# Delta rule: diagonal squares in the merges of the triangular inverse, and gate rows spread by transfers

## The chip, the cores and the metric

The kernel runs on one core of a Trainium2 chip. TensorE (PE) multiplies matrices, VectorE (DVE), ScalarE (ACT) and GpSimd (POOL) work on elements, SyncE (SP) issues transfers; each engine works through its own instructions in order and waits on semaphores. The metric is the device time of one execution in microseconds (us), lower is better. TensorE reads its operands from SBUF (128 partitions) and writes to PSUM, which has eight banks in every partition; a matmul smaller than the array takes only a square or rectangle of it, named by its rows and columns (128*128, 64*64, 16*16 in the profile's rows).

## The reference

Two transformer blocks over 256 tokens of width 1024, all in float32. The first has stick-breaking attention, an MLP, retention and another MLP. The second puts 16 meta tokens in front (272 tokens), and mixes with two branches, a gated delta rule and a forgetting attention, and ends with a layer of experts that are gathered from memory. The change lies in the gated delta rule. Cut to what matters, per head:

```python
G = jnp.cumsum(g, axis=-1)
gamma = jnp.where(incl, jnp.exp(G[:, None] - G[None, :]), 0.0)
k_beta = k * beta[..., None]
a_mat = jnp.where(strict, k_beta @ k.T * gamma, 0.0) + jnp.eye(CHUNK)
rhs = jnp.concatenate([v * beta[..., None], k_beta * jnp.exp(G)[..., None]], axis=-1)
sol = triangular_solve(a_mat, rhs, left_side=True, lower=True, unit_diagonal=True)
q_dec = q * jnp.exp(G)[..., None]
```

## The kernel before, in words

The weights stream from memory in 1 MB blocks of 128x2048 float32, issued by SP in `sync_blocks` (L576) into two slots in turn. ACT makes the upper part of each half-block (`weights_hi`, L602), DVE the rest (`weights_lo`, L611), and PE multiplies in three products (L625, L626, L627). SP may issue block b only when DVE has made the lower part of block b-2, since it goes to the same slot.

The delta rule comes after the convolution (`conv` blocks) and works on 8 heads in 2 groups of 4, over three token tiles of 16, 128 and 128 tokens (`TILES`). `tensor_delta`, `scalar_delta`, `vector_delta` and `gpsimd_delta` are the four engines' shares of it, written out in order by hand. Between the steps stand numbered fill points: at those in `DELTA_POINTS` each engine does half a block of the projections that the forgetting attention, the gates and so on need (24 matmuls of PE into bank 7). In group 0 no fill stands at points 10, 12, 16, 18 and 25; in group 1, of points 9 to 19, only at 14 and 17. Fill point 6+2L lies between the two products of level L, and 7+2L behind them.

The gates' rows G, beta and exp(G) lie in `lam`, one head to a partition (0 to 7), 272 tokens along it. ACT copies six of its rows to partitions 32, 64 and 96 (`scalar_spread`, three transfers). In each group PE spreads each of the three rows over all 128 partitions with a matmul by a 0/1 matrix (`tensor_pick`, L1586; four heads, on four row tiles and in four banks), and DVE reads it from PSUM: `dgam` (L2076), `dkb` (L2086), `dlast` and `dqe` (L2090, L2091).

The unit lower triangular matrix of each 128-token tile is inverted by merging: at level L, blocks of size 2^L on the diagonal are joined in pairs. A level does, for each tile and head, a transpose (L1952), the product M of the masked matrix `dB` and the second halves of `dTT` (L1959, 64 moving columns), copies of M and of the transpose to SBUF by ACT (L2044, L2046), the product Z (L1970), and a subtraction by DVE (L2130) into `dTT`; POOL masks `dA` into `dB` for the next level when M has been made (L2179). The products use the whole 128x128 array, although only squares on the diagonal carry anything. Level 6, the last, works on 64x64 quarters (L1950, L1957, L1968, `whole`). The 16-token tile (names ending in m) takes part up to level 3.

## Time and profile before

| | us |
|---|---|
| median of 3 runs | 1841.1 (1838.98 to 1842.49) |
| profiled execution | 1846.39 |
| its span | 1845.1 |
| PE busy | 1705.1 (92%) |
| DVE busy | 1187.9 (64%) |
| ACT busy | 752.1 (41%) |
| POOL busy | 400.0 (22%) |
| L1959 on the whole array, x160 | 20.1 |
| L1970 on the whole array, x160 | 20.1 |
| L1586 in the delta rule, x48 | 4.4 |

A float32 matmul appears as two records on PE, each of the three products of a half-block as one. The delta rule lies between about 806 and 1000 us of the span. Busy time is the time with something of that group running; the distance from one group's start to the next is what it takes on the engine. The clock that a window shows is 1.00 for TensorE's upper level (2.4 GHz) and 0.50 for its lower (1.2 GHz).

### The profile page before, as it was taken

The numbers are of one execution on the slowest core, as the hardware profiler recorded it, in microseconds if no ns is written. First come the engines' busy times: TensorE is split into PE (matmuls) and PEld (weight loads), VectorE is DVE, ScalarE is ACT, GpSimd is POOL, SyncE is SP. The second block draws the span as 40 slices with busy tenths as digits, with TensorE's granted clock in tenths as the row PEclk, the third lists the DMA queues.
The fourth block names the chain that finished last, engine by engine and source line by source line (L and its number), as shares of the span: only waits on it lengthen the run. The fifth ranks groups of instructions, "written<-read, shape, count | busy, mean of one in ns | idle before, by whom it ended". The sixth has DMA issues, their size and how long they took to land.

```text
span 1845.1 us, 23154 instructions
## 1 busy us (share of the span) xinstructions
PE 1705.1 (92%) x9262; PEld 1296.8 (70%) x9262; DVE 1187.9 (64%) x2131; ACT 752.1 (41%) x1324; POOL 400.0 (22%) x343
## 2 busy tenths in 40 slices
PE   8999999999999999999999999988788788878888
PEld 7979988977799888989999989863333333333333
DVE  5676654765566547864262666689777766777855
ACT  4655533444355436774363655442222121122211
POOL 0220000000000000002012000335545544544551
PEclk9999999999999999999899999998989878988899
DMA  6336555444455553532231224799999999999997
GB/s 252 135 117 213 189 184 183 176 167 160 160 182 184 183 183 137 183 118 79 82 115 47 107 100 173 283 382 418 422 421 421 422 421 421 422 421 421 421 422 311
DMA packets 62955, 453.85 MB, mean 246 GB/s; under 512 B 7000, under 2 KB 7128, under 8 KB 8448
## 3 DMA queue, kind: packets, MB, share of 16 engines
q0 software_dynamic: 37152, 268.45, 35.1%
q1 hardware_dynamic: 25040, 178.27, 27.0%
q10 hardware_dynamic: 656, 5.66, 0.9%
q8 instruction: 73, 1.20, 0.3%
q14 instruction: 34, 0.28, 0.0%
HBM read 451.15 MB, written 1.05 MB: 245 GB/s over the span
## 4 chain that ended last, share of the span: by engine, by line
PE 68%; DMA 14%; DVE 8%; ACT 4%; POOL 3%; issue 2%; another core or an unknown queue 0%; DVEq 0%; ACTq 0%; POOLq 0%
PE banks L625 16%; PE banks L627 16%; PE banks L626 16%; DMA uv_rows<-expert_uv,index 14%; PE banks L2539 10%; DVE uv_rows L2725 3%; POOL uv_rows L2755 3%; ACT weights_hi L602 1%; PE banks L1970 1%; PE banks L1959 1%; DVE weights_lo L611 1%; PE banks L1690 1%; PE banks L1952 1%; ACT diag L2604 1%; PE banks L2313 0%
## 5 line engine op out<-in xcount | busy, mean ns | idle before, releaser
L2539 PE MATMUL banks<-uv_rows,diag 128*128 128x512 f32 x1024 | 509.0, 660 | 110.2 <-ACT diag L2604 110.2
L611 DVE TENSOR_TENSOR weights_lo<-weights,weights_hi 128x1024 fp32r<-128x1024 f32 x325 | 397.1, 1263 | 252.0 <-ACT weights_hi L602 252.0
L2539 PEld LDWEIGHTS banks<-uv_rows,diag 128*128 128x128 f32 x1024 | 214.6, 213 | 403.2 <-issue 273.1
L602 ACT ACTIVATE weights_hi<-weights 128x1024 fp32r<-128x1024 f32 x328 | 328.9, 1052 | 357.4 <-PE banks L627 340.9
L625 PE MATMUL banks<-x_hi,weights_hi 128*128 128x256 f32 (+1 forms) x1472 | 426.6, 290 | 5.0 <-DVE weights_lo L611 1.4
L627 PE MATMUL banks<-x_hi,weights_lo 128*128 128x256 f32 (+1 forms) x1472 | 419.7, 285 | 0.0
L626 PE MATMUL banks<-x_lo,weights_hi 128*128 128x256 f32 (+1 forms) x1472 | 419.3, 285 | 0.0
L2725 DVE CUSTOM_DVE_ANT_0 uv_rows<-uv_rows,tokens 128x1024 f32<-128x1024 f32 x256 | 305.5, 1223 | 147.1 <-DMA uv_rows<-expert_uv,index 147.0
L2755 POOL DMA_INDIRECT uv_rows<-expert_uv,index x254 | 315.5, 1242 | 309.2 <-PE banks L2539 256.1
L625 PEld LDWEIGHTS banks<-x_hi,weights_hi 128*128 128x128 f32 x1472 | 281.1, 191 | 12.1 <-DVE weights_lo L611 3.1
L627 PEld LDWEIGHTS banks<-x_hi,weights_lo 128*128 128x128 f32 x1472 | 280.9, 191 | 0.0
L626 PEld LDWEIGHTS banks<-x_lo,weights_hi 128*128 128x128 f32 x1472 | 280.0, 190 | 0.5 <-issue 0.2
L2598 ACT ACTIVATE coef<-act_in 128x8 f32<-128x8 f32 (+3 forms) x43 | 8.9, 207 | 375.4 <-DVE act_in L2725 375.4
L625 PE MATMUL banks<-weights_hi,mlp_hi 128*128 128x512 f32 x256 | 101.2, 395 | 0.0
L627 PE MATMUL banks<-weights_hi,mlp_lo 128*128 128x512 f32 x256 | 101.0, 395 | 0.0
L626 PE MATMUL banks<-weights_lo,mlp_hi 128*128 128x512 f32 x256 | 101.0, 395 | 0.0
L2604 ACT ACTIVATE diag<-sb_now,coef 128x128 f32<-128x128 f32 x256 | 79.5, 388 | 14.7 <-DVE coef L2735 14.7
L835 POOL TENSOR_SCALAR stat<-stat 128x1 f32<-128x1 f32 x6 | 1.2, 207 | 357.4 <-DVE stat L813 357.2
L625 PE MATMUL banks<-weights_hi,x_hi 128*128 128x512 f32 x160 | 65.6, 410 | 1.8 <-DVE weights_lo L611 1.8
L626 PE MATMUL banks<-weights_lo,x_hi 128*128 128x512 f32 x160 | 63.4, 397 | 0.0
L627 PE MATMUL banks<-weights_hi,x_lo 128*128 128x512 f32 x160 | 63.4, 396 | 0.0
L627 PEld LDWEIGHTS banks<-weights_hi,mlp_lo 128*128 128x128 f32 x256 | 48.2, 188 | 11.2
(384 smaller groups left out, 2073.4 us busy)
## 6 DMA issues: line engine op xcount, KB each, us to landing
weights<-weights SPq DMA_DIRECT2D x164, 1024.0 KB, 4.8
uv_rows<-weights SPq DMA_DIRECT2D x4, 1024.0 KB, 7.7
uv_rows<-expert_uv,index POOLq DMA_INDIRECT x254, 17.5
sb_first<-constants_first ACTq DMA_DIRECT2D x1, 1920.0 KB, 9.5
sb_always<-constants_always ACTq DMA_DIRECT2D x1, 1627.5 KB, 7.2
sb_peer<-constants_peer ACTq DMA_DIRECT2D x1, 1544.0 KB, 8.0
h<-x SPq DMA_DIRECT2D x1, 1024.0 KB, 5.8
out<-h SPq DMA_DIRECT2D x4, 256.0 KB, 4.6
```

The lines of the kernel that those rows point to most:

```text
L602: self.act.activation(self.w_hi[b % SLOTS][:, f], raw[:, f], ACT.Copy).then_inc(self.hi_made, 1)
L611: self.dve.tensor_tensor(self.w_lo[b % SLOTS][:, f], self.landing(b)[0][:, f], self.w_hi[b % SLOTS][:, f], ALU.subtract).then_inc(self.lo_ ...
L625: self.pe.matmul(out, wh, xh, start=first, stop=False)
L626: self.pe.matmul(out, wh, xl, start=False, stop=False)
L627: return self.pe.matmul(out, wl, xh, start=False, stop=last)
L1690: mm = self.pe.matmul(self.bank(2 * (c % 3) + j, width), self.C["ones"][:, :], squares[:, j, :], start=True, stop=True)
L1952: pe.transpose(turned[:, hh * n:(hh + 1) * n], tt[:, hh, :], C["ident"][0:n, 0:n])
L1959: mm = pe.matmul(ps[:, hh], b[:, hh, :], self.second(tt, lvl)[:, hh], start=True, stop=True)
L2539: mm = pe.matmul(self.bank(2 * t + half), self.diag[:, k, :], self.uv[ROW_BUFFER[n]][:, f], start=(u < NT and k == 0), stop=(u >= UNITS - ...
L2604: act.activation(self.diag[:, k, :], self.C["ident"][:, :], ACT.Copy, scale=self.coef[:, u, k:k + 1]).then_inc(self.diags, 1)
L2725: dve.tensor_tensor_reduce(rows, rows, self.tokens[:, t, :], 1.0, 0.0, ALU.mult, ALU.add, self.act_in[:, u, k:k + 1]).then_inc(self.dots, 1)
L2755: pool.indirect_dma_start(self.uv[ROW_BUFFER[n]][:, :], None, self.ins["expert_uv"], bass.IndirectOffsetOnAxis(ap=self.index[:, u, k:k + 1 ...
```

## The change

In `tensor_delta`, levels 2 to 5 of the two 128-token tiles (`parted`) do M and Z as squares on the diagonal: at levels 2, 3 and 4 four squares of 32x32 with 16 moving columns, at level 5 two of 64x64 with 32. All squares of a head write one bank, each its own partitions. Level 1, level 6, the transposes and the 16-token tile stay.

The rows of G, beta and exp(G) are spread by SP instead (`sync_spread`): in each group, for each of the four heads, one transfer takes beta and G (2176 bytes of one partition) to all 128 partitions of the new buffer `drows`, and one takes exp(G) (1088 bytes) to rows of `lam` that are no longer needed. They stand ahead of one weight block each time (`SPREAD_AT`). The picks in the delta rule are gone; DVE reads the rows from SBUF and waits until all eight transfers of the group have landed. ACT copies only one row now (`ncum`, for the forgetting attention), in one transfer. `drows` lies where the gates' first half will be, so ACT's first gates fill waits for DVE's last read of it.

```diff
--- before.py
+++ after.py
@@ -194,6 +194,8 @@
           ("ret_out", 8), ("mlp_up1", 16), ("mlp_down1", 16), ("conv", 12), ("fa_qkv", 12), ("delta_z", 4),
           ("gates", 8), ("branch_a", 4), ("branch_b", 4), ("mix_out", 4), ("queries", 8))
 N_BLOCKS = sum(n for _, n in STREAM)
+CONV_AT = sum(n for _, n in STREAM[:10])
+SPREAD_AT = (CONV_AT + 9, CONV_AT + 12 + 8)
 HALVES = {"sb_v": 2, "sb_out": 2, "mlp_down0": 2, "ret_out": 2, "mlp_down1": 2, "mix_out": 2}
 SQUARES = (("sb", 1, 1), ("mlp0", 1, 1), ("ret", 1, 1), ("mlp1", 1, 1), ("meta", 1, 0), ("peer", 1, 1))
 ROOTS = (("sb", 2), ("ret", 2), ("meta", 1), ("mixer", 2), ("final", 2), ("peer", 2))
@@ -380,6 +382,9 @@
         self.branch.append([self.place(f"branch_{n}1", [P, KD, SM], F32R) for n in ("hi", "lo")])
         self.top = at
         self.fa_qkv = self.place("fa_qkv", [P, 3 * H2, SM])
+        at = self.top
+        self.d_rows = self.place("drows", [P, HG, 2, SM])
+        self.top = at
         self.y[0], self.y[1] = self.place("gates_a", [P, KD, S]), self.y[0]
@@ -573,6 +578,8 @@
                 self.sync_ahead(own + 1)
             if b >= SLOTS:
                 self.sp.wait_ge(self.lo_made, PARTS * (b - SLOTS + 1))
+            if b in SPREAD_AT:
+                self.sync_spread(SPREAD_AT.index(b))
             self.sp.dma_start(self.raw[b % SLOTS][:, :], w[b]).then_inc(self.block_full[b % SLOTS], 16)
         self.sync_ahead(own + 2)
         self.sync_ahead(own + 3)
@@ -1572,13 +1579,32 @@
     def row(self, name):
         return self.lam[0:H2, self.LAM.index(name), :]
-    LAM = ("beta", "G", "nbe", "tail", "eG", "ncum", "y", "t", "u", "g")
+    LAM = ("nbe", "tail", "beta", "G", "eG", "ncum", "y", "t", "u", "g")
+    SPREAD = 16 * 2 * HG
+
+    def sync_spread(self, group):
+
+        sp, beta, eg, kept = self.sp, self.LAM.index("beta"), self.LAM.index("eG"), self.LAM.index("ncum") + 1
+        if group == 0:
+            sp.wait_ge(self.lam_ready, 1)
+            sp.wait_ge(self.lam_eg, 1)
+            sp.wait_ge(self.h_normed, NT)
+        else:
+            sp.wait_ge(self.d["rows_used"].sem, self.d["rows_used"].at(0, 3))
+        for hh in range(HG):
+            h = group * HG + hh
+            sp.dma_start(self.d_rows[:, hh], self.lam[h:h + 1, None, beta:beta + 2, :].to_broadcast([1, P, 2, SM])).then_inc(self.rows_spread, 16)
+            sp.dma_start(self.lam[:, kept + hh, :], self.lam[h:h + 1, None, eg, :].to_broadcast([1, P, SM])).then_inc(self.rows_spread, 16)
+
+    def rows_landed(self, group):
+
+        return self.rows_spread, 16 + (group + 1) * self.SPREAD
     def scalar_spread(self):
+        at = self.LAM.index("ncum")
         self.act.wait_ge(self.lam_ready, 1)
-        for j in range(1, 4):
-            self.act.dma_start(self.lam[j * QUARTER:j * QUARTER + H2, 0:6, :], self.lam[0:H2, 0:6, :]).then_inc(self.rows_spread, 16)
+        self.act.dma_start(self.lam[QUARTER:QUARTER + H2, at, :], self.lam[0:H2, at, :]).then_inc(self.rows_spread, 16)
     def tensor_pick(self, out, name, h, quarter, width, start=True):
@@ -1823,6 +1849,16 @@
         return t > 0 and lvl == self.LEVELS[t] - 1
+    def parted(self, lvl, t):
+
+        return t > 0 and lvl > 1
+
+    def parts(self, lvl):
+
+        n = max(QUARTER, 2 << lvl)
+        for at in range(0, P, n):
+            yield slice(at, at + n), slice(at >> lvl + 1, at + n >> lvl + 1), slice(at // 2, (at + n) // 2)
+
     def level_count(self, lvl, t):
         return sum(len(self.active(l)) for l in range(1, lvl)) + self.active(lvl).index(t) + 1
@@ -1861,6 +1897,8 @@
         name, s, sub, b = self.fill(i)
         c = 2 * s + sub
         act.wait_ge(*self.fill_made(i))
+        if name == "gates" and c == 0:
+            act.wait_ge(self.d["rows_used"].sem, self.d["rows_used"].at(1, 3))
         if name == "fa_qkv":
             act.activation(self.fa_qkv[:, c, :], self.bank(FILL_BANK, SM), ACT.Copy).then_inc(self.fill_moved, 1)
         elif name == "delta_z":
@@ -1898,17 +1936,9 @@
         def fill(point):
             self.fill_point(self.tensor_fill, group, point)
-        if group == 0:
-            pe.wait_ge(self.rows_spread, 16 * 3)
-        for j, name in enumerate(("G", "beta", "eG")):
-            if j:
-                wait("rows_used", j)
-            for hh in range(HG):
-                h = group * HG + hh
-                mm = self.tensor_pick(self.bank(hh, SM), name, h, hh, SM)
-            mm.then_inc(d["rows"].sem, 1)
+        for j in range(3):
             fill(j)
-        wait("rows_used", 3)
+        wait("rows_used", 2)
         if group == 0:
             pe.wait_ge(self.conv_silu, self.st["conv"].n)
         for t, (c, n) in enumerate(TILES):
@@ -1955,6 +1985,9 @@
                 for hh in range(HG):
                     if self.whole(lvl, t):
                         mm = pe.matmul(ps[0:half, hh, 0, :], a[half:P, hh, 0:half], tt[half:P, hh, half:P], start=True, stop=True)
+                    elif self.parted(lvl, t):
+                        for x, blocks, cols in self.parts(lvl):
+                            mm = pe.matmul(ps[x, hh, blocks], b[x, hh, x], self.second(tt, lvl)[x, hh, blocks], start=True, stop=True)
                     else:
                         mm = pe.matmul(ps[:, hh], b[:, hh, :], self.second(tt, lvl)[:, hh], start=True, stop=True)
                 mm.then_inc(d["M"].sem, 1)
@@ -1966,6 +1999,10 @@
                 for hh in range(HG):
                     if self.whole(lvl, t):
                         mm = pe.matmul(pzt[0:half, hh, 0, :], tm[0:half, hh, 0:half], m1[0:half, hh, 0:half], start=True, stop=True)
+                    elif self.parted(lvl, t):
+                        for x, blocks, cols in self.parts(lvl):
+                            mm = pe.matmul(pzt[x, hh, blocks], tm[x, hh, x], m1[x, hh, cols].rearrange("p (b s) -> p b s", s=1 << lvl),
+                                           start=True, stop=True)
                     else:
                         mm = pe.matmul(pzt[:, hh], tm[:, hh, :], m1[:, hh, 0:n // 2].rearrange("p (b s) -> p b s", s=1 << lvl),
                                        start=True, stop=True)
@@ -2027,8 +2064,8 @@
             act.wait_ge(d["turn"].sem, d["turn"].at(group, t + 1))
             for hh in range(HG):
                 h, f = group * HG + hh, slice(hh * P, (hh + 1) * P)
-                act.activation(self.d_ktail[0:n, t, f], self.bank(2)[0:n, f], ACT.Copy, scale=self.token_scalar(t, 3, h))
-                made = act.activation(self.d_bv[0:n, t, f], self.bank(3)[0:n, f], ACT.Copy, scale=self.token_scalar(t, 0, h))
+                act.activation(self.d_ktail[0:n, t, f], self.bank(2)[0:n, f], ACT.Copy, scale=self.token_scalar(t, 1, h))
+                made = act.activation(self.d_bv[0:n, t, f], self.bank(3)[0:n, f], ACT.Copy, scale=self.token_scalar(t, 2, h))
             made.then_inc(d["turn_used"].sem, 1)
             fill(3 + t)
             act.wait_ge(d["back"].sem, d["back"].at(group, t + 1))
@@ -2069,12 +2106,12 @@
         def fill(point):
             self.fill_point(self.vector_fill, group, point)
-        rows = self.banks(0, HG, SM)
-        wait("rows", 1)
+        beta, rows = self.d_rows[:, :, 0, :], self.lam[:, self.LAM.index("ncum") + 1:, :]
+        dve.wait_ge(*self.rows_landed(group))
         for t, (c, n) in enumerate(TILES):
             for hh in range(HG):
-                g = dve.tensor_scalar(self.d_gam[0:n, hh, c:c + n], self.bank(hh)[0:n, c:c + n],
-                                      self.token_scalar(t, 1, group * HG + hh), 0.0, ALU.subtract, ALU.min)
+                g = dve.tensor_scalar(self.d_gam[0:n, hh, c:c + n], self.d_rows[0:n, hh, 1, c:c + n],
+                                      self.token_scalar(t, 3, group * HG + hh), 0.0, ALU.subtract, ALU.min)
                 if (t, hh) != (2, HG - 1):
                     step.of(g)
         g.then_inc(d["rows_used"].sem, 1)
@@ -2082,10 +2119,10 @@
             for i in CONV_FILLS:
                 self.vector_fill(i)
         fill(0)
-        wait("rows", 2)
-        dve.tensor_tensor(self.d_kb[:, :, :], k, rows, ALU.mult).then_inc(d["rows_used"].sem, 1)
+        if group == 0:
+            dve.wait_ge(self.rms_scaled.sem, self.rms_scaled.at("conv", 8))
+        dve.tensor_tensor(self.d_kb[:, :, :], k, beta, ALU.mult).then_inc(d["rows_used"].sem, 1)
         fill(1)
-        wait("rows", 3)
         for t, (c, n) in enumerate(TILES):
             step.of(dve.tensor_copy(last[:, :, t:t + 1], rows[:, :, c + n - 1:c + n]))
         dve.tensor_tensor(self.d_qe[:, :, :], q[:, :, META:SM], rows[:, :, META:SM], ALU.mult).then_inc(d["rows_used"].sem, 1)
@@ -2291,6 +2328,7 @@
         for i in range(H2 + 2):
             if i < H2:
                 if i == 0:
+                    pe.wait_ge(*self.rows_landed(1))
                     pe.wait_ge(self.rms_read.sem, self.rms_read.at("outs", 12))
                     pe.wait_ge(self.rms_scaled.sem, self.rms_scaled.at("outs", 8))
                 if i >= 2:
```

PE at level 2 of group 0, before (`dTTm`, `dMm` belong to the 16-token tile; a row with x3 counts matmuls of the other heads; 1959 is M, 1952 the transpose, 1970 Z):

```order
L1952 MATMUL banks<-sb_now,dTT 128x128 [waits d_T]
L1952 MATMUL banks<-sb_now,dTT 128x128 x3
L1959 MATMUL banks<-dTT,dB 128x64 [waits d_B]
L1959 MATMUL banks<-dTT,dB 128x64 x3
L1970 MATMUL banks<-dMm,dTm 16x8 [waits d_M1]
L1970 MATMUL banks<-dMm,dTm 16x8 x3
L1970 MATMUL banks<-dM,dT 128x64 [waits d_M1]
L1970 MATMUL banks<-dM,dT 128x64 x3
```

The same place after (M is L1990, the transpose L1982, Z L2004):

```order
L1982 MATMUL banks<-sb_now,dTT 128x128 [waits d_T]
L1982 MATMUL banks<-sb_now,dTT 128x128 x3
L1990 MATMUL banks<-dTT,dB 32x16 [waits d_B]
L1990 MATMUL banks<-dTT,dB 32x16 x15
L2007 MATMUL banks<-dMm,dTm 16x8 [waits d_M1]
L2007 MATMUL banks<-dMm,dTm 16x8 x3
L2004 MATMUL banks<-dM,dT 32x16 [waits d_M1]
L2004 MATMUL banks<-dM,dT 32x16 x15
```

Each set of 4 matmuls has become one of 16; what stands around them, and what they wait for, is as it was.

SP at the first spread, after; before, the two weight blocks (`weights_49` and `weights_50` are the two slots) follow each other with a wait for `block_lo_made` each:

```order
L583 DMA weights_49<-weights 128x2048 [waits block_lo_made]
L1596 DMA drows<-lam 128x1x544 [waits lam_eg,h_normed,lam_ready,block_lo_made]
L1597 DMA lam<-lam 128x1x272
L1596 DMA drows<-lam 128x1x544
L1597 DMA lam<-lam 128x1x272
L1596 DMA drows<-lam 128x1x544
L1597 DMA lam<-lam 128x1x272
L1596 DMA drows<-lam 128x1x544
L1597 DMA lam<-lam 128x1x272
L583 DMA weights_50<-weights 128x2048
```

Eight transfers stand between two blocks, and the first waits for the gates' rows; the block that used to be next is now behind them in the same queue.

PE at the first pick of group 0, before:

```order
L627 MATMUL banks<-x_hi,weights_lo_54 128x272
L1586 MATMUL banks<-lam,sb_always 128x272 [waits rows_spread,rms_read]
L1586 MATMUL banks<-lam,sb_always 128x272 x3
L625 MATMUL banks<-x_hi,weights_hi_52 128x272 [waits half_blocks_moved]
L626 MATMUL banks<-x_lo,weights_hi_52 128x272
L627 MATMUL banks<-x_hi,weights_lo_54 128x272
```

And after, where the products (L632 to L634) follow one another:

```order
L632 MATMUL banks<-x_hi,weights_hi_52 128x272
L633 MATMUL banks<-x_lo,weights_hi_52 128x272
L634 MATMUL banks<-x_hi,weights_lo_54 128x272
L632 MATMUL banks<-x_hi,weights_hi_52 128x272 [waits half_blocks_moved,rms_read]
L633 MATMUL banks<-x_lo,weights_hi_52 128x272
L634 MATMUL banks<-x_hi,weights_lo_54 128x272
```

The four picks and their wait for `rows_spread` are gone, and the wait for bank 7 stands with the product.

## Rows read from the trace of the kernel before

**Rows 1.** The page: busy time, chain of waits, one kind of transfer.

```profile
PE 1705.1 (92%) x9262; PEld 1296.8 (70%) x9262; DVE 1187.9 (64%) x2131; ACT 752.1 (41%) x1324; POOL 400.0 (22%) x343
...
GB/s 252 135 117 213 189 184 183 176 167 160 160 182 184 183 183 137 183 118 79 82 115 47 107 100 173 283 382 418 422 421 421 422 421 421 422 421 421 421 422 311
...
PE 68%; DMA 14%; DVE 8%; ACT 4%; POOL 3%; issue 2%; another core or an unknown queue 0%; DVEq 0%; ACTq 0%; POOLq 0%
...
weights<-weights SPq DMA_DIRECT2D x164, 1024.0 KB, 4.8
```

**Rows 2.** Windows: stretch, length, busy time and count by engine, granted clock, DMA share, GB/s.

```profile
813.30:816.70 3.40, 3.40 (x17) 3.40 (x16) 2.85 (x3) 2.27 (x4) 0.00 (x0) 0.50 0.86 299
892.00:895.10 3.10, 2.09 (x27) 1.63 (x25) 0.00 (x0) 2.92 (x6) 0.00 (x0) 1.00 0.00 0
895.10:902.00 6.90, 6.90 (x38) 6.78 (x39) 3.10 (x4) 0.43 (x2) 0.00 (x0) 0.51 0.16 46
998.80:1004.40 5.60, 4.82 (x55) 3.97 (x55) 0.83 (x2) 2.26 (x6) 0.00 (x0) 1.00 0.52 187
```

**Rows 3.** Timeline of PE, group 1, level 2: start, length, engine, line, operation, tile, count.

```profile
975.12 0.61 PE L1952 MATMUL banks<-sb_now,dTT 128*128 128x128 f32 x4
975.56 1.00 PE L1959 MATMUL banks<-dTT,dB 128*128 128x64 f32 x8
976.49 0.35 PE L1970 MATMUL banks<-dMm,dTm 16*16 16x8 f32 x8
976.78 2.00 PE L1970 MATMUL banks<-dM,dT 128*128 128x64 f32 x16
978.71 0.26 PE L1952 MATMUL banks<-sb_now,dTTm 16*16 16x16 f32 x4
```

**Rows 4.** Timeline, group 0, level 2: ScalarE's copies and GpSimd's masks.

```profile
859.04 2.56 POOL L2179 TENSOR_TENSOR dB<-dA,sb_always 128x512 f32<-128x512 f32 x2 [1.12 <-PE banks L1959]
...
859.28 0.59 ACT L2046 ACTIVATE dT<-banks 128x512 f32<-128x512 f32 x1
...
860.56 0.59 ACT L2046 ACTIVATE dT<-banks 128x512 f32<-128x512 f32 x1
```

**Rows 5.** Timeline of PE, group 0, level 6.

```profile
892.41 0.68 PE L1957 MATMUL banks<-dTT,dA 64*64 64x64 f32 x8
893.02 0.41 PE L1950 MATMUL banks<-sb_now,dTT 64*64 64x64 f32 x4
```

**Rows 6.** Windows of 0.02 us: L978 (two column tiles, one bank).

```profile
67.70:67.72 0.02, 0.02 (x2) 0.02 (x2) 1.00 1.54 410
```

**Rows 7.** Windows of 0.02 us: L1586 (four row tiles, four banks).

```profile
806.52:806.54 0.02, 0.02 (x4) 0.02 (x4) 1.00 0.00 0
```

**Rows 8.** Timeline of PE at the second and third row spread, group 0.

```profile
812.73 0.39 PE L625 MATMUL banks<-x_hi,weights_hi 128*128 128x272 f32 x1 [1.41 <-DVE weights_lo L611]
...
817.47 0.74 PE L1586 MATMUL banks<-lam,sb_always 8*128 8x272 f32 x8
818.14 0.39 PE L625 MATMUL banks<-x_hi,weights_hi 128*128 128x272 f32 x1
```

**Rows 9.** Timelines of SP, ACT and PE: two weight blocks from issue to use.

```profile
756.36 0.33 SPq L576 DMA_DIRECT2D weights<-weights  x1
...
764.76 2.01 ACT L602 ACTIVATE weights_hi<-weights 128x1024 fp32r<-128x1024 f32 x2 [0.30 <-PE banks L627]
...
770.91 0.29 PE L625 MATMUL banks<-x_hi,weights_hi 128*128 128x272 f32 x1
...
845.48 0.33 SPq L576 DMA_DIRECT2D weights<-weights  x1
...
865.86 1.99 ACT L602 ACTIVATE weights_hi<-weights 128x1024 fp32r<-128x1024 f32 x2
```

**Rows 10.** Transfers, 756.0 to 757.2: only lam's copy moves.

```profile
DMA packets 19, 0.05 MB, mean 44 GB/s; under 512 B 11, under 2 KB 11, under 8 KB 19
...
weights<-weights SPq DMA_DIRECT2D x1, 1024.0 KB, 6.0
```

More of the change, by code:

```diff
@@ L525, in signals @@
         self.rows_spread = nc.alloc_semaphore("rows_spread")
-        names = {"rows": 3, "rows_used": 3, "gam": 3, "prod": 3, "prod_used": 3, "turn": 3, "turn_used": 3, "masked": 3, "attn": 2,
+        names = {"rows_used": 3, "gam": 3, "prod": 3, "prod_used": 3, "turn": 3, "turn_used": 3, "masked": 3, "attn": 2,
                  "back": 3, "A": 3, "T0": 3, "B": 13, "M": 15, "M1": 15, "Z": 15, "T": 15, "ks": 2,
@@ L2139, in vector_delta @@
                 for hh in range(HG):
-                    x = dve.scalar_tensor_tensor(self.d_rhs[:, H[hh]], ks[:, H[hh]], self.token_scalar(t, 2, group * HG + hh),
+                    x = dve.scalar_tensor_tensor(self.d_rhs[:, H[hh]], ks[:, H[hh]], self.token_scalar(t, 0, group * HG + hh),
                                                  self.d_bv[:, t, H[hh]], ALU.mult, ALU.add)
```

## The prediction

> **What bounds the kernel now.** I read the page first: PE is busy for 1705.1 of the span and carries 68% of the chain of waits [rows 1], so a microsecond taken from PE's row is a microsecond of the kernel unless something else arrives late there. Then the windows around the delta rule: PE is full in most of it, and the exceptions are level 6 of the inverse, where it is busy for 2.09 of 3.10 us and for 4.82 of 5.60 us [rows 2]. The reader should see in the same group that the granted clock stands at 0.51 for the 6.90 us behind the first of these, and at 0.50 for 3.40 us at 813.3: the lower of the two levels, after a stretch in which PE paused or stood. Last the timelines: how long one set of a level takes on PE, and when ScalarE and GpSimd deliver what the next set needs.
>
> **The squares.** Five steps give the sum.
>
> First, a whole-array set of 4 matmuls (8 records): the second M set of level 2 runs from 975.56 to 976.49, 0.93, and the two Z sets from 976.78 to 978.71, 0.965 each [rows 3]. I take 0.95. Its busy time of 1.00 is not its price, since the next group starts before it ends.
>
> Second, a set of quarters is 16 matmuls, four to each of four squares. The trace of before has no such thing. If the four squares run beside one another, each does what the 16-token tile does in 976.49 to 976.78, 0.29 for 8 records, and [rows 3] gives its busy time as 0.35; I take 0.35, which leaves something for changing the tile form. That they can start together is what L1586 shows: four matmuls on four row tiles have all begun within 0.02 us, PE busy with x4 [rows 7]. If they run one after another, a set costs 4 x 0.29 = 1.16. There are 3 levels x 2 tiles x 2 products x 2 groups = 24 such sets: 24 x (0.95 - 0.35) = 14.4 gained; at the other end 24 x (1.16 - 0.95) = 5.0 lost.
>
> Third, a set of halves: a 64x64 set of the same 8 records takes from 892.41 to 893.02, 0.61 [rows 5], with 64 moving columns where the new ones have 32. Two squares side by side: 0.61; one after another 1.22. 1 x 2 x 2 x 2 = 8 sets: 8 x (0.95 - 0.61) = 2.7 gained, or 8 x (1.22 - 0.95) = 2.2 lost.
>
> Fourth, what is late then. Between M and Z, ScalarE copies dM and dT of each tile; its dT copies end at 859.87 and 861.15 [rows 4], 1.28 apart, and before that distance is covered by PE's own sets. With quarters PE has done the second tile's transposes (975.12 to 975.56, 0.44 [rows 3], which stay) and M (0.35) long before. Counting on from the first M set: dT of the first tile is ready about 1.3 after that set started, PE is there at 1.15 with the small tile's Z; dT of the second is ready at about 2.15, PE is there at 1.6. So 0.7 of standing, plus a little for DVE's subtraction before the next transposes: 0.85 at each level that has no fill between M and Z, which are levels 2, 3 and 5 of both groups: 6 x 0.85 = 5.1 given back. At level 4 the fill of 24 matmuls hides it. The ends are 0 (ScalarE starts its copies earlier by all that PE is earlier) and 6 x 1.28 = 7.7 (PE stands through a whole pair of copies). GpSimd's two masks, 2.56 for a level [rows 4], start with the M of the level before and fit into a level of about 3.9; were that cover gone, each level would cost the difference to 2.56 and nothing more.
>
> So the squares give 14.4 + 2.7 - 5.1 = 12.0.
>
> Fifth, the clock. PE's standing in these levels is what came before the lower level at 895.10 and 1004.40 [rows 2]. Levels 2 and 3 of group 1 have no fill at all. One stretch at the lower level cost, in the window at 813.30, 17 records in 3.40 us; at the upper level fills of this width are 0.13 apart (in [rows 9] the record at 770.91 is one of such a row), so 17 x 0.13 = 2.2 and 1.2 lost. At most it is half of the 6.90 us at 895.10, 3.4. I expect two more such stretches at 2.2 each, near the middle: 4.4. Ends: none, and six at 2.2, 13.2.
>
> **The picks.** 24 matmuls go. In group 0 the second is followed by a product that waited for VectorE's lower part until 812.73 in any case [rows 8], and the first has the same kind of wait behind it, so these give nothing. The third holds PE from 817.47 to 818.14: 0.67 [rows 8]. In group 1 I count one of three the same way, 0.67, and nothing for the rest, where ScalarE's copy of the fill before ends late. VectorE's gam, now from SBUF, saves a few tenths on an engine with room. Together 1.3; the ends are 0 and 6 x 0.67 = 4.0.
>
> **The transfers.** In each group 4 x 128 x (2176 + 1088) bytes = 1.67 MB are written ahead of a weight block, and the block lands that much later. At the best pace that the page shows, 422 GB/s [rows 1], they take T = 4.0. How much delay is covered: the first block is issued at 756.36 and landed 6.0 later [rows 9, 10], at 762.4; PE first needs it at 770.9, and its upper parts take 2.0 and the first lower part about 1.0 as well, so some 5 are free. The second is issued at 845.48, lands 4.8 later [rows 1] at 850.3, and ScalarE splits it only at 865.86 [rows 9], so 15 are free. SP needs 8 x 0.33 = 2.6 for the issues, inside T. With T = 4.0 everything is hidden, by 1 us at the first place. The other end for T comes from the only copy on the chip that before has: lam's rows, 0.05 MB in a window of 1.2 us in which nothing else moves, 44 GB/s, from 8 partitions [rows 10]. That gives T = 38. Behind the waiting SP stand only weight blocks, and for these ScalarE, VectorE and PE. I take the first end, as these transfers write all 128 partitions as the weight blocks do; the other end is a rival below. The gates fill's new wait for `drows` and DVE's wait for all eight transfers are met long before: DVE reads them at about 807, 50 us after the first spread.
>
> **The sum.** 12.0 + 1.3 - 4.4 = 8.9 less. The profiled execution has 1846.4, its span 1845.1 and 1.3 around it; it lies 5.3 above the median of 1841.1. So 1846.4 - 8.9 = 1837.5 for an execution like the profiled one, and 1832.2 against the median.
>
> **Rivals.**
>
> The transfers are slow, because all 128 rows of one are read from one partition. Price: T = 38 stalls PE by 38 - 5 = 33 at the first place and 38 - 15 = 23 at the second, 56 in all: 1832.2 + 56 = 1888.2, slower. It begins to show from T = 5, and turns the gain into a loss from about T = 14. For it: eight packets of 6528 bytes moved no faster than 44 GB/s with all engines idle [rows 10]. Against it: that copy is small, so that what is fixed in a transfer weighs heavily. The Trainium skill ("SBUF — State Buffer", Door 1: The DMA port swizzle) says that a transfer's rate depends on how many of 16 ports its partitions reach, gives 27.6 GB/s for partitions 0 to 3, which share one, and 1.67 MB at that rate would be an estimate of 61 us, or 1932 in the end; no run here shows which side of a copy it binds, but 44 GB/s for 8 partitions, which reach two ports by that rule, fits it. Because of that fit this case gets a large chance.
>
> The squares do not run beside one another. Then PE loses 5.0 + 2.2 = 7.2, no wait comes free, the clock stays as it was, and the picks still give 1.3: 1841.1 + 7.2 - 1.3 = 1847.0, slower. For it: all four squares of a head write the same bank, while the four row tiles of L1586 write four banks [rows 7]. Against it: the two column tiles of L978, which write one bank, have both begun within 0.02 us [rows 6]. The Trainium skill ("TensorEngine Tiling (Array Packing)", Gotcha 1: PSUM Pressure) says that different row tiles cannot access the same PSUM bank simultaneously; the new squares differ in rows and columns at once, and no row of before shows such a pair.
>
> The clock takes it. With six stretches at the lower level, 13.2 in place of 4.4, the time is 1832.2 + 8.8 = 1841.0. For it: both windows with PE not full are followed by or near one at half clock [rows 2]. Against it: the levels of group 0 have a fill after each Z.
>
> **Chances.** Forecast 0.42, slow transfers 0.30, no side by side 0.13, clock 0.15. The forecast's own range is 1826 to 1838, from the ends of the waits and of the clock that are near it. What this kernel's times can tell from no change is 0.2%, 3.7 us: faster is under 1837.4. Faster: 0.40 of the forecast, 0.04 of the clock's case, 0.01 of slow transfers; 0.45. Same: 0.02, 0.10, 0.02 and 0.02 of slow transfers; 0.16. The rest, 0.39, is slower. The range to hold 8 in 10 goes from 1824 to 1889: below lie 0.03, above the part of the slow transfers that are slower than lam's copy, 0.16.
>
> **What would show it.** On the page of the changed kernel: M and Z groups of 32*32 with a distance of 0.3 to 0.4 for 32 records (right), or above 1.0 (not side by side). ScalarE's dT copy as the releaser of Z at levels 2, 3 and 5, for 0.85 a level. The granted clock in the windows of levels 2 to 5. SP's eight issues, the time from the first of them to the landing of the last, and an idle stretch of PE with SP's weight block as its releaser a few us later: with T near 4 there is none; one of over 20 us at both places proves my choice of T wrong, and with it the sign.

## The result and the profile after

The changed kernel takes 1943.2 us (median of 4 runs, 1942.61 to 1944.13), the kernel before in the same comparison 1841.8; the ratio is 1.0542, 95% interval [1.0529, 1.0555]. It is 101 us slower, where I had forecast 9 faster. The profiled execution took 1942.61, its span 1941.3.

The page of the changed kernel, busy time and chain of waits (columns as in [rows 1]):

```profile
PE 1686.8 (87%) x9854; PEld 1282.7 (66%) x9854; DVE 1186.5 (61%) x2131; ACT 751.6 (39%) x1324; POOL 400.9 (21%) x343
...
PE 64%; DMA 16%; DVE 7%; SPq 5%; ACT 4%; POOL 2%; issue 1%; ACTq 0%; DVEq 0%; POOLq 0%
```

PE has 18 us less to do and is still later. New in the chain is SPq with 5%: time in SP's queue, which no chain of before had. The waits of PE in the stretch of the first spread and the second (engine and line, what ended the wait, us in all, times, longest):

```profile
PE banks L632 <- DVE weights_lo L618: 57.4, 2, 55.9
PE banks L2007 <- ACT dTm L2083: 29.6, 1, 29.6
PE banks L632 <- issue: 13.1, 1, 13.1
```

These are two places. PE stands 55.9 us until VectorE has split a weight block, and later 13.1 and 29.6 us, one behind the other, within group 0's levels: 98.6 us together. Behind the 55.9 and the 29.6 stands ScalarE, which splits each block first and itself waited for one to land (in the second case ahead of its copy of dTm):

```profile
821.82 2.00 ACT L609 ACTIVATE weights_hi<-weights 128x1024 fp32r<-128x1024 f32 x2 [58.55 <-DMA weights<-weights]
...
967.04 2.00 ACT L609 ACTIVATE weights_hi<-weights 128x1024 fp32r<-128x1024 f32 x2 [30.62 <-DMA weights<-weights]
```

In the 13.1 the wait has no semaphore behind it (issue). A load of 16 KB of code for PE ran from 932.67 to 933.60 in it, and PE went on at 934.95. The two places hold nearly the whole loss. Behind each wait PE also starts again at the lower clock, first in the window below (columns as in [rows 2]), then at 0.50 from 935.0 to 939.7 and 0.56 from 969.3 to 978.0:

```profile
825.40:833.00 7.60, 7.60 (x44) 7.60 (x45) 7.16 (x14) 5.25 (x9) 0.00 (x0) 0.69 0.66 218
```

That is some 17 us at the lower level, by half of them an estimate of 8.5 us lost. With it the loss is 107 us, of which the squares and the picks give a part back.

What they wait for stands in SP's timeline (start, length, engine, line):

```profile
755.16 0.56 SPq L1596 DMA_DIRECT2D drows<-lam  x1
...
756.40 7.61 SPq L1596 DMA_DIRECT2D drows<-lam  x1
764.06 5.14 SPq L1597 DMA_DIRECT2D lam<-lam  x1
769.24 10.28 SPq L1596 DMA_DIRECT2D drows<-lam  x1
779.56 5.14 SPq L1597 DMA_DIRECT2D lam<-lam  x1
784.75 10.29 SPq L1596 DMA_DIRECT2D drows<-lam  x1
795.07 5.14 SPq L1597 DMA_DIRECT2D lam<-lam  x1
800.26 10.29 SPq L583 DMA_DIRECT2D weights<-weights  x1
```

From the fourth transfer on, SP's entries have their steady length, 10.28 + 5.14 us for a pair (the third took 7.61). That is 278,528 bytes in 10.28 us, 27.1 GB/s, and the 8 transfers of a group take 4 x 15.4 = 61.7 us; their pieces moved from 756.4 to 818.5, 62.1. The transfers' view between 760 and 815 says the same for all 16 engines together:

```profile
DMA packets 1003, 1.47 MB, mean 27 GB/s; under 512 B 112, under 2 KB 543, under 8 KB 1003
...
q1 hardware_dynamic: 1003, 1.47, 87.3%
```

The transfer engines are busy for 87% of that time and move 27 GB/s. The page before has 422 at best [rows 1]; that is the stretch in which the experts' rows are gathered, not the weight blocks' own pace. The Trainium skill ("SBUF — State Buffer", Door 1: The DMA port swizzle) gives 27.6 GB/s for four partitions on one port; the trace agrees with 27.1, here for reading from one partition.

The squares did what was hoped of them. PE in group 1, level 2, to be set beside [rows 3]:

```profile
1070.35 0.25 PE L1982 MATMUL banks<-sb_now,dTTm 16*16 16x16 f32 x4
...
1070.81 0.66 PE L1982 MATMUL banks<-sb_now,dTT 128*128 128x128 f32 x4
1071.40 0.44 PE L1990 MATMUL banks<-dTT,dB 32*32 32x16 f32 x32
1071.77 0.66 PE L1982 MATMUL banks<-sb_now,dTT 128*128 128x128 f32 x4
1072.36 0.44 PE L1990 MATMUL banks<-dTT,dB 32*32 32x16 f32 x32
1072.63 0.34 PE L2007 MATMUL banks<-dMm,dTm 16*16 16x8 f32 x8
1072.84 0.44 PE L2004 MATMUL banks<-dM,dT 32*32 32x16 f32 x32
1073.80 0.44 PE L2004 MATMUL banks<-dM,dT 32*32 32x16 f32 x32 [0.52 <-ACT dT L2083]
1074.17 0.26 PE L1982 MATMUL banks<-sb_now,dTTm 16*16 16x16 f32 x4
```

A set of quarters, 32 records, takes 0.37 us (1071.40 to 1071.77), where 8 records on the whole array took 0.93. A level takes 1070.35 to 1074.17, 3.82 us. Before it was 5.39, to 978.71 from this row:

```profile
973.32 0.25 PE L1952 MATMUL banks<-sb_now,dTTm 16*16 16x16 f32 x4
```

Between the two Z sets of the changed kernel PE stands 0.5 for ScalarE's dT.

### The profile page after: what moved, and what is told of

It is laid out like the page before. It is cut to its first block, busy times and chain, and to the rows that moved or that the text cites. A ratio compares the mean times of both kernels' runs of the same rounds, so it can differ in the third digit from the quotient of the medians.

```text
span 1941.3 us, 24356 instructions
## 1 busy us (share of the span) xinstructions
PE 1686.8 (87%) x9854; PEld 1282.7 (66%) x9854; DVE 1186.5 (61%) x2131; ACT 751.6 (39%) x1324; POOL 400.9 (21%) x343
## 4 chain that ended last, share of the span: by engine, by line
PE 64%; DMA 16%; DVE 7%; SPq 5%; ACT 4%; POOL 2%; issue 1%; ACTq 0%; DVEq 0%; POOLq 0%
PE banks L632 15%; PE banks L634 15%; PE banks L633 15%; DMA uv_rows<-expert_uv,index 14%; PE banks L2577 10%; SPq L1596 3%; DVE uv_rows L2763 2%; DMA weights<-weights 2%; POOL uv_rows L2793 2%; SPq L1597 2%; ACT weights_hi L609 1%; DVE weights_lo L618 1%; PE banks L1716 1%; ACT diag L2642 1%; PE banks L1982 0%
## 5 line engine op out<-in xcount | busy, mean ns | idle before, releaser
L2577 PE MATMUL banks<-uv_rows,diag 128*128 128x512 f32 x1024 | 498.5, 649 | 120.0 <-ACT diag L2642 120.0
L632 PE MATMUL banks<-x_hi,weights_hi 128*128 128x256 f32 (+1 forms) x1472 | 430.7, 293 | 76.6 <-DVE weights_lo L618 57.4
L634 PE MATMUL banks<-x_hi,weights_lo 128*128 128x256 f32 (+1 forms) x1472 | 422.8, 287 | 0.0
L632 PEld LDWEIGHTS banks<-x_hi,weights_hi 128*128 128x128 f32 x1472 | 284.2, 193 | 83.1 <-DVE weights_lo L618 59.0
L634 PEld LDWEIGHTS banks<-x_hi,weights_lo 128*128 128x128 f32 x1472 | 284.5, 193 | 0.0
L632 PE MATMUL banks<-weights_hi,mlp_hi 128*128 128x512 f32 x256 | 101.2, 395 | 0.0
L634 PE MATMUL banks<-weights_hi,mlp_lo 128*128 128x512 f32 x256 | 101.0, 395 | 0.0
L632 PE MATMUL banks<-weights_hi,x_hi 128*128 128x512 f32 x160 | 64.9, 405 | 1.8 <-DVE weights_lo L618 1.8
L634 PE MATMUL banks<-weights_hi,x_lo 128*128 128x512 f32 x160 | 62.9, 393 | 0.0
```

Source lines behind the costliest of these rows:

```text
L632: self.pe.matmul(out, wh, xh, start=first, stop=False)
L634: return self.pe.matmul(out, wl, xh, start=False, stop=last)
L2577: mm = pe.matmul(self.bank(2 * t + half), self.diag[:, k, :], self.uv[ROW_BUFFER[n]][:, f], start=(u < NT and k == 0), stop=(u >= UNITS - ...
```

## The experiments

Times are medians, and intervals are 95% intervals of the ratio to the kernel before on the same chip. There were 14 runs: twelve kernels, and two repeated profiles (`before_again`, `merges_again`) of one execution each. Code is cut to the lines that matter; `...` marks where lines of the same change are left out.

**Which half of the change.** `merges` has the squares alone:

```diff
+                    elif self.parted(lvl, t):
+                        for x, blocks, cols in self.parts(lvl):
+                            mm = pe.matmul(ps[x, hh, blocks], b[x, hh, x], self.second(tt, lvl)[x, hh, blocks], start=True, stop=True)
...
```

> The squares alone: levels 2 to 5 as in the changed kernel, the gates' rows by TensorE's picks and lam's three copies as before. Theory: the squares run beside one another (32 records in 0.37 us in the changed kernel's trace against 0.93 for 8 of the whole array) and a level 2 of group 1 takes 3.8 us instead of 5.4, so about 12 us less with at most 4 given back by the clock: 1830 to 1834. Rival (the clock takes it): level times shrink, but further stretches at half clock in the fills behind levels cost as much, 1838 to 1842.

Measured: 1846.5 us against 1843.4, ratio 1.0019 [1.0009, 1.0030]. That is neither the theory's 1830 to 1834 nor the rival's 1838 to 1842, but a little slower than no change. `transfers` has the rest of the change alone:

```diff
     def parted(self, lvl, t):
-        return t > 0 and lvl > 1
+        return False
```

> The transfers alone: everything of the change but the squares. Theory: the two stalls of PE behind the weight blocks (55.9 and 42.7 us in the changed kernel) are the whole loss, so this is slower than the changed kernel by what the squares give, 1950 to 1957. Rival (the squares have a part in the loss): it comes out faster than the changed kernel's 1943.

Measured: 1950.1 us, ratio 1.0585 [1.0557, 1.0612]. The transfers make the whole loss, in the same two places (PE's waits there are 55.7 and 45.7 us, the second here for ScalarE alone). Beside them the squares gave 6.9 us (about 8 by the ratios), alone they cost 3.

**What limits the transfers.** Both kernels fill partitions 64 to 127 from a second copy of the row, one (`two_same`, below) at partition 32+h, the other (`two_other`, with `half * 64`) at 64+h:

```diff
+            for half in range(2):
+                to, at = slice(half * P // 2, (half + 1) * P // 2), h + half * 32
+                sp.dma_start(self.d_rows[to, hh], self.lam[at:at + 1, None, beta:beta + 2, :].to_broadcast([1, P // 2, 2, SM])).then_inc(self.rows_spread, 16)
+                sp.dma_start(self.lam[to, kept + hh, :], self.lam[at:at + 1, None, eg, :].to_broadcast([1, P // 2, SM])).then_inc(self.rows_spread, 16)
...
```

> The changed kernel with ACT copying lam's first six rows to partitions 32 and 64 as before, and each spread made as two transfers: to partitions 0 to 63 from partition h, to 64 to 127 from partition 32+h. Theory (a port that partitions h and 32+h share, read at 27 GB/s): a group's spread still takes 61 to 62 us, time about 1943. Rival 1 (a single partition is the limit): it takes 31 us, time about 1883. Rival 2 (writing 128 partitions in pieces of 1 or 2 KB is the limit, or a cost per piece): 61 us as well, so this run does not tell it from the theory, the next does.

> As the run before it, but partitions 64 to 127 are filled from partition 64+h. Theory (a port each): the halves run beside each other, a group's spread takes 31 us, PE stands 31-5=26 and 31-15=16 us, 60 less than the changed kernel: about 1883 to 1890. Rival 1 (a single partition): the same 31 us. Rival 2 (a cost per piece or of writing): still 61 us and about 1943.

The transfers' view of `two_same` (765 to 805) and of `two_other` (765 to 795):

```profile
DMA packets 834, 1.08 MB, mean 27 GB/s; under 512 B 166, under 2 KB 511, under 8 KB 834
```

```profile
DMA packets 915, 1.21 MB, mean 40 GB/s; under 512 B 182, under 2 KB 540, under 8 KB 915
```

`two_same`: 27 GB/s and 1945.4 us, ratio 1.0559 [1.0532, 1.0586], as the change. Two partitions 32 apart are no better than one, so the single partition is not the limit. `two_other`: 40 GB/s and 1913.4 us, ratio 1.0386 [1.0359, 1.0412]. Only the place of the source differs between the two, so neither the pieces of 1 and 2 KB nor the writing was the limit at 27 GB/s. A shared way out of partitions h and 32+h is, and 64+h has another. I had expected twice the rate and 31 us. It was 1.5 times in this window, and the pieces of the whole spread moved from 758.4 to 803.5, 45 us. The two halves stand behind one another in one queue and may overlap only in part; no run tests that.

**By way of memory.** `bounce` is the whole change, but ACT writes the three rows of all heads (26 KB) to device memory and SP spreads them from there, at the same places:

```diff
+        self.act.dma_start(self.ins["scratch"][:, :, :], self.lam[0:H2, beta:beta + 3, :]).then_inc(self.rows_spread, 16)
...
+        heads = slice(group * HG, (group + 1) * HG)
+        kept_rows = self.ins["scratch"][heads, :, :]
+        sp.dma_start(self.d_rows[:, :, :, :], kept_rows[None, :, 0:2, :].to_broadcast([P, HG, 2, SM])).then_inc(self.rows_spread, 16)
+        sp.dma_start(self.lam[:, kept:kept + HG, :], kept_rows[None, :, 2, :].to_broadcast([P, HG, SM])).then_inc(self.rows_spread, 16)
```

> The whole change, but the rows go by way of device memory: ACT writes lam's rows beta, G and exp(G) (26 KB) to memory in one transfer, and SP's spread of a group is two transfers from there to 128 partitions, at the same places ahead of the same weight blocks. Theory (reading one partition's port is the limit): the two spreads take 4 to 8 us each, both stalls are gone, and the time is that of the squares alone less a little for the picks, 1843 to 1847. Rival (writing 1.67 MB in pieces of one partition, or the place in SP's queue, is what costs): the spreads still take tens of us, over 1870.

Measured: 1837.5 us, ratio 0.9979 [0.9967, 0.9991], faster than the 1843 to 1847 expected. The same 1.67 MB go to the same 128 partitions in the same 1024 pieces of 2176 and 1088 bytes. Issued at 756.2, the last piece had landed at 764.1, 7.9 us later; the next weight block's pieces begin at 763.0. Between 755.5 and 763 the transfers' view reads:

```profile
DMA packets 962, 1.60 MB, mean 213 GB/s; under 512 B 18, under 2 KB 449, under 8 KB 961
```

PE's longest wait for a weight block between 740 and 1000 is now 1.5 us (in the kernel before 1.4). `bounce_rows` is this without the squares (`parted` returns False).

> The rows by way of device memory without the squares: products on the whole array as before. Theory (the picks cost about 1.3 us, the way through memory is hidden): 1840 to 1843, so that of the 5.9 us that rows and squares gained together most belongs to the squares. Rival (the picks cost more than their own time, since TensorE's order around them loosens): 1837 to 1839, and the squares give next to nothing.

Measured: 1841.6 us, ratio 0.9987 [0.9974, 0.9999]. The picks' removal gives 2 us or so, and the interval overlaps that of `bounce`, so the squares' part in `bounce` is not told apart from nothing.

**Another queue.** `pool_queue` has the sixteen transfers of the change issued by GpSimd:

```diff
-            if b in SPREAD_AT:
-                self.sync_spread(SPREAD_AT.index(b))
...
+        self.gpsimd_spread(0)
+        self.gpsimd_delta(0)
+        self.gpsimd_spread(1)
```

> The changed kernel with its sixteen transfers issued by GpSimd instead of SP: group 0's before its first mask, group 1's after group 0's masks; sources and bytes as in the change. Theory 1 (the weight blocks stand only because they are behind the spread in one queue): no stall at the weight blocks, the first group's rows (wanted about 50 us later) 10 us late at most, the second's some 10 to 15 us late, 1850 to 1870. Theory 2 (the 16 transfer engines are held up whatever the queue): the weight blocks stand as long as in the changed kernel, 1930 to 1950.

Measured: 1918.8 us, ratio 1.0399 [1.0380, 1.0418]; between the theories, nearer the second. PE's waits, 740 to 1000:

```profile
PE banks L631 <- DVE weights_lo L617: 39.5, 4, 25.9
PE banks L632 <- issue: 36.7, 1, 36.7
```

The weight blocks still come late (39.5 us in four waits in place of 57.4 in two), though SP's queue holds nothing but weights. The transfers' view between 760 and 820, with the spread in q0 and the weights in q1:

```profile
q0 software_dynamic: 420, 1.34, 73.0%
q1 hardware_dynamic: 595, 4.35, 17.9%
```

The spread takes 73% of the 16 transfer engines' time, and it is no quicker: its pieces, here of 4352 bytes, moved from 748.8 to 811.7, 62.9 us. So neither the size of the pieces nor the queue sets its pace. At the second spread PE stands 36.7 us for no semaphore: no load of code lies between 916.7 and 970.4 in the trace, and PE goes on at 972.7, behind the latter. I read both as transfer engines that all queues share, code loads included; a queue of its own takes away a quarter of the loss (74 us in place of 101).

**Where the squares' gain goes.** The windows over the levels of group 0 and of group 1 (columns as in [rows 2]), first the kernel before:

```profile
850.00:900.00 50.00, 48.92 (x437) 47.32 (x436) 14.65 (x23) 18.70 (x39) 8.02 (x8) 0.95 0.18 64
950.00:1010.00 60.00, 57.93 (x533) 55.26 (x532) 25.07 (x34) 27.19 (x64) 15.83 (x13) 0.97 0.20 71
```

then `merges`:

```profile
850.00:900.00 50.00, 45.10 (x753) 41.46 (x752) 14.65 (x23) 18.60 (x39) 7.83 (x7) 0.87 0.20 68
950.00:1010.00 60.00, 56.25 (x857) 51.00 (x856) 24.36 (x34) 26.68 (x60) 15.73 (x13) 0.89 0.21 72
```

A mean clock of 0.87 over 50 us is 13 us at the lower level, 0.89 over 60 is 13 more: 26 against 5 + 4 = 9 of before. At half the clock such a stretch does half the work, so an estimate of what is lost is half of the difference, 8.5 us. In the timeline of `merges` at level 2 of group 0 a set of quarters breaks off for 2.0 us with no wait; a load of code ran from 859.58 to 860.50, and PE went on 1.4 us after it:

```profile
859.63 0.27 PE L1984 MATMUL banks<-dM,dT 32*32 32x16 f32 x12
...
861.90 0.29 PE L1984 MATMUL banks<-dM,dT 32*32 32x16 f32 x3 [2.00 <-issue]
```

To tell whether this is the program's or chance, both kernels were profiled once more:

> The kernel before, profiled once more, for the spread between profiles: the same four stretches at the lower clock level (17 us in all) if they are set by the program, other ones if by chance.

> The squares alone, profiled once more. If the 34 us at the lower clock level are the program's, 27 to 34 again, and a code load that comes 2 us late in level 2 of group 0; if they are chance, about 10 to 20, as in the other kernels.

`before_again`, then `merges_again`:

```profile
850.00:900.00 50.00, 48.92 (x441) 47.33 (x440) 14.65 (x23) 18.85 (x40) 8.56 (x8) 0.97 0.19 66
950.00:1010.00 60.00, 57.77 (x532) 55.01 (x532) 23.94 (x36) 26.00 (x57) 15.82 (x13) 0.97 0.21 71
```

```profile
850.00:900.00 50.00, 45.11 (x752) 41.46 (x751) 14.66 (x23) 18.59 (x39) 7.82 (x7) 0.87 0.20 68
950.00:1010.00 60.00, 56.32 (x848) 51.38 (x847) 24.30 (x36) 25.50 (x57) 15.74 (x13) 0.86 0.20 72
```

It is the program's: 0.97 and 0.97 against 0.87 and 0.86, and the break of 2.0 us is there again at 859.6. By these two the same estimate gives (30 - 7) / 2, about 12 us. The times of these single executions, 1844.1 and 1842.6, are within the spread of both kernels.

`warm` gives PE something to do where it stands:

```diff
+                for _ in range(2 if self.whole(lvl, t) and t == 1 else 1 if t == 2 and lvl in (2, 3, 5) else 0):
+                    pe.matmul(self.level_bank(t, 2)[:, 0:2 * P], C["ident"][:, :], self.t_now[:, 0:2 * P], start=True, stop=True)
```

> The squares alone, with idle work for TensorE where it stands: one product of 128x256 that nobody reads ahead of the second tile's Z at levels 2, 3 and 5, and two ahead of the first tile's Z at level 6. It adds up to 8 x 0.45 us of TensorE work, nearly all in places where it stood. Theory (the lower clock level, 34 us of the squares' trace against 17 of before, takes the gain): the time at the lower level falls to about 17 us and the kernel to 1838 to 1841. Rival (the clock is not set by these stands, or the code load at level 2 decides): as the squares alone, 1846 to 1848, or slower by the added work.

Measured: 1837.3 us, ratio 0.9972 [0.9961, 0.9983]. Contrary to what I wrote, these products are read: the subtraction takes the whole 256 columns and relies on the zeros that level 1 left beside the squares. So this kernel's output is wrong, and only its time counts. There are ten such products, each about 0.65 us on PE in the trace of `warm_free`, and not eight of 0.45. `warm_free` writes to columns 256 to 511 of the bank instead, which nobody reads:

> The squares alone with the same idle products as in the run called warm, but into the free half of the bank. Theory (these products keep the clock up): as warm, 1836 to 1840, with some 10 us at the lower level. Rival (warm's gain was chance, or came from what it wrote): as the squares alone, 1845 to 1848.

Measured: 1838.0 us, ratio 0.9972 [0.9962, 0.9982]. Its windows:

```profile
850.00:900.00 50.00, 46.86 (x780) 41.69 (x779) 14.65 (x23) 19.28 (x41) 7.83 (x7) 0.97 0.21 69
950.00:1010.00 60.00, 57.27 (x878) 51.30 (x877) 23.27 (x33) 26.14 (x58) 15.71 (x13) 0.94 0.21 74
```

More work, and the kernel is 8 us faster than `merges`, whose interval lies wholly above 1. The clock is at 0.97 and 0.94, about 10 us at the lower level in place of 26, although the break for code (2.6 us at 859.9) is there as well. So the clock took most of the squares' gain, and what it took comes back when PE is kept at work. It is not all: with the clock where it was before, the squares bring 5.2 us and not the 12.0 of my sum. 2.6 of the rest is the break; how much the idle products' own time takes was not separated.

`halves` has 64x64 squares at all of levels 2 to 5:

```diff
-        n = max(QUARTER, 2 << lvl)
+        n = max(2 * QUARTER, 2 << lvl)
```

> The squares alone, but as halves (64x64, 32 moving columns) at all of levels 2 to 5: 8 matmuls a set instead of 16. A set takes about 0.55 us instead of 0.3 and level sets lose 24 x 0.25 = 6 us of the gain, but TensorE has fewer instructions to fetch in a short time. Theory 1 (an instruction fetch that comes too late, 2.0 us at level 2 of group 0, and the clock that falls with it, cost about 5): no idle time with the releaser issue there, about 12 us less at the lower level or less, and 1841 to 1845. Theory 2 (the clock alone, whatever the fetch): 1845 to 1849.

Measured: 1838.5 us, ratio 0.9971 [0.9959, 0.9983], better than both theories: larger squares, 8 us faster than the quarters alone. No break for code is in its trace, and in the same two windows its clock is 0.93 and 0.97, near that of before. The one run does not tell which of the two counts for how much. `bounce`, with quarters, has no break either, and 0.93 and 0.89: this goes with its gain of 7 us on `merges` (by the ratios), of which the picks' 2 are a part.

**The best of it.** `bounce_warm` is `bounce` with the idle products of `warm_free`; `bounce_halves_warm` also has `halves`.

> Rows by way of memory, the squares in quarters as in the change, and the idle products for TensorE (one of 128x256 ahead of the second tile's Z at levels 2, 3 and 5, two ahead of level 6), now into the free half of the bank, so that nothing they write is read. Theory (clock): less time at the lower level than the 24 us of the same kernel without them, and 1831 to 1835. Rival (the idle products only add work): 1838 to 1840.

> As the run before it, with halves (64x64) in place of the quarters at levels 2 to 4. Theory (a steady clock and fewer instructions are worth as much as the smaller squares): within 2 us of the run before it. Rival (the quarters' shorter sets count in full, 24 x 0.25 us): 4 to 6 us slower than it.

Measured: 1832.3 us, ratio 0.9931 [0.9918, 0.9945], and 1835.4 us, 0.9945 [0.9932, 0.9959]. Both beat the kernel before and the changed one. The windows of `bounce_warm`:

```profile
850.00:900.00 50.00, 49.44 (x798) 44.14 (x797) 14.65 (x23) 20.01 (x43) 7.83 (x7) 0.97 0.31 111
950.00:1010.00 60.00, 57.72 (x896) 52.33 (x895) 22.64 (x39) 24.88 (x51) 13.66 (x11) 0.97 0.21 72
```

With the clock kept up the quarters are as good as the halves or better; the intervals overlap.

## Why the prediction was wrong

**The transfers' pace, the step that failed.** I took T = 4.0 "as these transfers write all 128 partitions as the weight blocks do", and left T = 38 from lam's copy [rows 10] to a rival. T is 61.7. The 422 GB/s behind 4.0 were not the weight blocks' but the pace at which the experts' rows are gathered; even when read from device memory, in `bounce`, the same bytes took 7.9 us. That was hidden, since PE's longest wait for a block is 1.5 there and 1.4 before. The rest, 7.9 to 61.7, is the source. I looked at where a transfer writes and not at where it reads: the weight blocks are read from device memory, these rows from one partition, and `two_same`, `two_other` and `bounce` show that the source decides. The rival had the mechanism and, by the Trainium skill's figure, nearly the size (61 us; the sum by its own terms is 1934, not 1932, and 1943.2 was measured). I counted it at 0.30 and kept the page's figure out of the range, whose end of 1889 came from the faster pace of a copy out of 8 partitions. That those 8 lie on two ports instead of one is a statement of the Trainium skill ("SBUF — State Buffer", Door 1: The DMA port swizzle); no run here varied it.

**The cover, right at the first place, 4 short at the second.** I had 5 us free at the first place and 15 at the second. Measured: 61.7 - 55.9 = 5.8, and 61.7 - 42.7 = 19. With T = 61.7 my own formula gives 57 + 47 = 103; the two stalls were 98.6.

**The squares side by side, right.** 0.35 a set was forecast, 0.27 to 0.37 measured, in one bank. The Trainium skill ("TensorEngine Tiling (Array Packing)", Gotcha 1: PSUM Pressure) says different row tiles cannot access the same PSUM bank simultaneously. Here the squares of a head differ in row and column tile and write disjoint partitions of one bank, and 32 records take 0.37 us, so that case is not bound by it. Not in my sum: the whole-array transposes between them take 0.59 each (1070.81 to 1071.40) instead of 0.44 to 0.50.

**The waits behind them, over-sized.** 0.85 a level was forecast, 0.5 is in the trace. All in all a level is at 3.8 us, where I had 3.9.

**The clock, under-sized.** I gave it 4.4 us and 13.2 at worst. In `merges` it took 8.5 to 12 by the two estimates, and a late load of code 2.0, which I had not thought of. This is the part of the forecast that would have been wrong even with quick transfers: `merges` has 1.0019, and `bounce` is 0.2% faster than before (3.9 us) where I had forecast 8.9. The account does not close: 12.0 gained less 8.5 to 12 and 2.0 would leave `merges` between 1.5 faster and 2 slower, and it is 3.5 slower by its ratio. What the remaining 1.5 to 5 us are stays open.

**The picks.** 1.3 was forecast; `bounce_rows` has 0.2 to 4.8 less by its interval (0.9999 to 0.9974), which holds it.

## What to carry to other kernels

For a transfer ask where it reads as well as where it writes: rows of one partition of SBUF came out at 27 GB/s, to 128 partitions, with 16 transfer engines busy and from either of two queues; a second source 32 partitions away changed nothing, one 64 away gave 40. A trip through device memory for 26 KB made the same spread eight times quicker (7.9 us for 61.7). A transfer put ahead of a stream that has little slack costs its whole length less that slack, and in another queue still the larger part of it (74 of 101 us here). And work taken from TensorE in small pieces can be paid back in clock: look at the granted clock of the stretch before counting the gain, and try idle products, or larger pieces, where it fell.

## What the runs showed of the hardware

- 16 transfer engines were busy for 87% of the time at 27 GB/s. Other queues' transfers came late beside it (weight blocks 39.5 us in `pool_queue`), and PE stood 36.7 us there in a stretch without a load of code.
- SP itself is held: from the fourth transfer on, issuing one takes as long as one takes to run, 10.28 and 5.14 us.
- In sets of 32x32 products (32 records in 0.27 us) PE broke off for 2.0 us with no semaphore to wait for, around a load of code 0.92 us long, at the same place in both profiles of `merges`. `bounce` has the same sets and no such break, so the density alone does not do it. Each of the four breaks looked at (`after`, `pool_queue`, `merges`, `warm_free`) ended 1.35 to 1.44 us after the end of such a load; that the load is what ended it is my reading.
- Diagonal squares of 32x32 in different rows and columns of the array ran together into one bank: 32 records in 0.27 to 0.37 us, where four squares one after another would take 4 x 0.29 = 1.16 by the 16-token tile's 0.29 [rows 3].
